# A fifth buffer for the high parts of the expert weights, and splits four tiles ahead of TensorE instead of three

## The reference

```python
logits = (h @ router).astype(jnp.float32)
top_v, top_i = lax.top_k(logits, TOP_K)          # 2 of 8 experts
gates = jax.nn.softmax(top_v, axis=-1)
...
for e in range(N_EXPERTS):
    y = y + gate_full[..., e:e + 1] * _swiglu(h, w_gate_up[e], w_down[e])
```

## Time and profile before

| what | value |
|---|---|
| median of 3 runs | 1521.85 us (1520.17 to 1522.1) |
| the profiled execution | 1522.17 us |
| its span, first to last instruction | 1520.2 us |
| busy share of the span: PE, PEld, DVE, ACT, POOL | 97%, 80%, 76%, 65%, 9% |
| granted clock of TensorE, mean | 0.998 |
| moved by DMA | 468.26 MB, mean 308 GB/s |
| item 0 begins on TensorE, item 7 ends | 617.2 us, 1508.6 us |

### The profile page before, as it was taken

The page is one execution under the profiler, slowest core; times in us unless marked ns, Lnnn a source line. Parts: engine busy times, 40 slices in busy tenths (PEclk is TensorE's granted clock), DMA queues, the critical chain, the costliest instruction groups (busy, mean ns, idle before and its releaser), DMA issues.

```text
span 1520.2 us, 19543 instructions
## 1 busy us (share of the span) xinstructions
PE 1481.3 (97%) x7678; PEld 1208.7 (80%) x7678; DVE 1158.3 (76%) x1021; ACT 991.1 (65%) x869; POOL 132.2 (9%) x137
## 2 busy tenths in 40 slices
PE   8999999999989999999999999999999999999996
PEld 6888888899969987888777788777888777888774
DVE  5555445454565456899899988899898999898997
ACT  5544434343453337777798777888776888776986
POOL 0000000006034314000000200000100000000000
PEclk9999999999999999999999999999999999999999
DMA  9655555567516653899999999999999999999996
GB/s 333 214 170 190 168 192 171 189 192 224 194 57 213 206 185 126 329 356 355 366 405 417 398 407 405 395 408 415 399 408 403 395 408 415 399 404 408 393 391 220
DMA packets 151056, 468.26 MB, mean 308 GB/s; under 512 B 9856, under 2 KB 15872, under 8 KB 138416
## 3 DMA queue, kind: packets, MB, share of 16 engines
q1 hardware_dynamic: 144784, 453.93, 79.8%
q0 software_dynamic: 2816, 9.96, 2.3%
q10 hardware_dynamic: 3360, 3.06, 0.7%
HBM read 459.55 MB, written 7.37 MB: 307 GB/s over the span
## 4 chain that ended last, share of the span: by engine, by line
PE 79%; DVE 13%; ACT 3%; DMA 1%; SPq 1%; issue 1%; DVEq 0%; ACTq 0%
DVE wlo L418 9%; PE bS L437 6%; PE bS L438 6%; PE bS L436 6%; PE bY L436 6%; PE bY L438 6%; PE bY L437 6%; PE bG L436 4%; PE bG L438 4%; PE bU L436 4%; PE bG L437 4%; PE bU L438 4%; PE bU L437 4%; DVE wlo_more L418 2%; ACT whi L412 2%
## 5 line engine op out<-in xcount | busy, mean ns | idle before, releaser
L418 DVE TENSOR_TENSOR wlo<-raw,whi 128x2048 fp32r<-128x2048 f32 x364 | 827.2, 2296 | 179.6 <-ACT whi L412 178.4
L412 ACT ACTIVATE whi<-raw 128x2048 fp32r<-128x2048 f32 x364 | 692.3, 1915 | 262.1 <-PE bS L438 118.2
L418 DVE TENSOR_TENSOR wlo_more<-raw_more,whi 128x2048 fp32r<-128x2048 f32 x60 | 136.4, 2288 | 10.7 <-ACT whi L412 10.6
L412 ACT ACTIVATE whi<-raw_more 128x2048 fp32r<-128x2048 f32 x60 | 114.5, 1914 | 28.0 <-DMA raw_more<-in_m_w_gate_up_dram 8.4
L1086 PE MATMUL bY<-whi,hTh 128*128 128x512 f32 x224 | 91.5, 408 | 6.9 <-DVE wlo L418 4.9
L436 PE MATMUL bY<-whi,hTh 128*128 128x512 f32 x224 | 89.8, 401 | 0.0
L437 PE MATMUL bY<-whi,hTl 128*128 128x512 f32 x224 | 89.1, 398 | 0.0
L437 PE MATMUL bS<-whi,eTl 128*128 128x512 f32 x192 | 76.4, 398 | 0.0
L436 PE MATMUL bS<-whi,eTh 128*128 128x512 f32 x192 | 76.4, 398 | 0.0
L1086 PE MATMUL bS<-whi,eTh 128*128 128x512 f32 x192 | 76.3, 398 | 0.0
L1087 PE MATMUL bY<-wlo,hTh 128*128 128x512 f32 x184 | 73.2, 398 | 0.0
(11 more groups left out here) (536 smaller groups left out, 3336.4 us busy)
## 6 DMA issues: line engine op xcount, KB each, us to landing
raw<-in_m_w_gate_up_dram SPq DMA_DIRECT2D x184, 1024.0 KB, 14.5
raw<-in_m_w_down_dram SPq DMA_DIRECT2D x90, 1024.0 KB, 14.4
raw_more<-in_m_w_gate_up_dram SPq DMA_DIRECT2D x40, 1024.0 KB, 14.6
raw<-in_b_w_in_dram SPq DMA_DIRECT2D x36, 1024.0 KB, 5.1
raw<-in_f_w_gate_up_dram SPq DMA_DIRECT2D x28, 1024.0 KB, 5.2
raw_more<-in_m_w_down_dram SPq DMA_DIRECT2D x20, 1024.0 KB, 14.2
raw<-in_f_w_down_dram SPq DMA_DIRECT2D x14, 1024.0 KB, 5.0
raw<-in_a_w_out_dram SPq DMA_DIRECT2D x4, 1024.0 KB, 16.8
```

Source lines behind the costliest of these rows:

```text
L412: nc.scalar.activation(whi[:, h], raw_of(r), ACT.Copy).then_inc(hi_done, 1)
L418: nc.vector.tensor_tensor(wlo_of(r), raw_of(r), whi[:, h].bitcast(F32), ALU.subtract).then_inc(lo_done, 1)
```

## The change

`whi` gets a fifth place, `whi_late`, in the memory of `hn`. The fifth place comes into use with tile `T_LATE + 1` = 97, that is tile 6 of item 0: until `T_LATE` = 96 the places go round by four, from there by five (`hi_slot`), and the wait for a free place looks back five tiles instead of four (`hi_free`). Tile 97's split also waits until `hn` has been stored and gathered from. In the experts ACT and DVE split tile t + 4 (`LEAD`) where they split tile t + 3, between the same small operations; one split of each (tile `T_MOE + 3`) is put ahead of item 0. SP's loops read the number of the next expert one tile later; the loads and their order are the same. Items beyond the eighth keep four places.

```diff
+LEAD = 4
@@ memory
+        top[0] = at_hn
+        whi_late = place("whi_late", [2048], F32R)
+        assert top[0] == phase
@@ places
+        T_LATE = -(-(T_MOE + HI + 1) // HI) * HI
+
+        def hi_slot(t):
+
+            return t % HI if t < T_LATE else (0, HI, 1, 2, 3)[(t - T_LATE) % (HI + 1)]
+
+        def hi_free(t, item):
+
+            if isinstance(item, int) and in_order(t, item) > T_LATE:
+                return used_count(t, item, HI + 1)
+            return used_count(t, item, HI)
+
+        whi_of = lambda h: whi[:, h] if h < HI else whi_late[:]
@@ slots
-                return ring(t), t % HI
+                return ring(t), hi_slot(t)
@@ make_hi
-                act.wait_ge(tile_used, used_count(t, item, HI))
-            nc.scalar.activation(whi[:, h], raw_of(r), ACT.Copy).then_inc(hi_done, 1)
+                act.wait_ge(tile_used, hi_free(t, item))
+            if isinstance(item, int) and in_order(t, item) == T_LATE + 1:
+                act.wait_ge(hn_out, 32)
+                act.wait_ge(gd_psum, 4)
+            nc.scalar.activation(whi_of(h), raw_of(r), ACT.Copy).then_inc(hi_done, 1)
@@ wblk_backward (what TensorE reads)
-            return backward(whi, h * 2048 + b * 512, HI * 2048), low
+            high = backward(whi, h * 2048 + b * 512, HI * 2048) if h < HI else backward(whi_late, b * 512, 2048)
+            return high, low
@@ SP
-            for t in range(FFN_TILES, FFN_TILES + CUT):
+            for t in range(FFN_TILES, FFN_TILES + LEAD):
...
-                for t in range(CUT, FFN_TILES):
+                for t in range(LEAD, FFN_TILES):
@@ ACT and DVE, ahead of item 0
             cut_tokens(0)
+            make_hi(act, T_MOE + LEAD - 1)
...
             ahead(T_MOE - 1)
+            make_lo(dve, T_MOE + LEAD - 1)
@@ full_item, and likewise half_item, of ACT and of DVE
-                        if not alone or t + CUT < FFN_TILES:
-                            make_hi(act, T_MOE + t + CUT, n)
+                        if not alone or t + LEAD < FFN_TILES:
+                            make_hi(act, T_MOE + t + LEAD, n)
```

More of the change, by code:

```diff
@@ L417, in make_lo @@
             dve.wait_ge(hi_done, count(item, FFN_TILES, t + 1))
-            nc.vector.tensor_tensor(wlo_of(r), raw_of(r), whi[:, h].bitcast(F32), ALU.subtract).then_inc(lo_done, 1)
+            nc.vector.tensor_tensor(wlo_of(r), raw_of(r), whi_of(h).bitcast(F32), ALU.subtract).then_inc(lo_done, 1)
         def wblk(t, b):
@@ L1420, in pre_tile_hi @@
                 r, h = slots(t, n)
-                act.wait_ge(tile_used, used_count(t, n, HI))
+                act.wait_ge(tile_used, hi_free(t, n))
                 act.wait_ge(pre_full, 16)
-                nc.scalar.activation(whi[:, h, 0:1024], raw_of(r)[:, 0:1024], ACT.Copy).then_inc(pre_hi, 1)
+                nc.scalar.activation(whi_of(h)[:, 0:1024], raw_of(r)[:, 0:1024], ACT.Copy).then_inc(pre_hi, 1)
                 act.wait_ge(*full_count(t, n))
-                nc.scalar.activation(whi[:, h, 1024:2048], raw_of(r)[:, 1024:2048], ACT.Copy).then_inc(hi_done, 1)
+                nc.scalar.activation(whi_of(h)[:, 1024:2048], raw_of(r)[:, 1024:2048], ACT.Copy).then_inc(hi_done, 1)
             def last_tile_hi(t, n):
                 r, h = slots(t, n)
-                act.wait_ge(tile_used, used_count(t, n, HI))
+                act.wait_ge(tile_used, hi_free(t, n))
                 for b in range(4):
@@ L1433, in last_tile_hi @@
                     sl = slice(b * 512, b * 512 + 512)
-                    nc.scalar.activation(whi[:, h, sl], raw_of(r)[:, sl], ACT.Copy).then_inc(last_hi if b < 3 else hi_done, 1)
+                    nc.scalar.activation(whi_of(h)[:, sl], raw_of(r)[:, sl], ACT.Copy).then_inc(last_hi if b < 3 else hi_done, 1)
             def turned_sel(n):
@@ L1485, in ahead @@
                     for t in tiles:
[L1486 to L1491, removed]
+                        if by_half and t + LEAD == FFN_TILES - 1:
+                            last_tile_hi(T_MOE + t + LEAD, n)
+                        elif by_half and t + LEAD == FFN_TILES - 2:
+                            pre_tile_hi(T_MOE + t + LEAD, n)
+                        elif not by_half or t + LEAD < FFN_TILES:
+                            make_hi(act, T_MOE + t + LEAD, n)
                 def copy_gate(j):
@@ L1588, in _ @@
                     y_right((m, 1, E - 1))
-                    for t in range(CUT):
+                    for t in range(LEAD):
                         make_hi(act, T_MOE + t, (m, 1, E))
@@ L2015, in pre_tile_lo @@
                 dve.wait_ge(pre_hi, 1)
-                nc.vector.tensor_tensor(wlo_of(r)[:, 0:1024], raw_of(r)[:, 0:1024], whi[:, h, 0:1024].bitcast(F32),
+                nc.vector.tensor_tensor(wlo_of(r)[:, 0:1024], raw_of(r)[:, 0:1024], whi_of(h)[:, 0:1024].bitcast(F32),
                                         ALU.subtract).then_inc(pre_lo, 1)
                 dve.wait_ge(hi_done, t + FFN_TILES * n + 1)
-                nc.vector.tensor_tensor(wlo_of(r)[:, 1024:2048], raw_of(r)[:, 1024:2048], whi[:, h, 1024:2048].bitcast(F32),
+                nc.vector.tensor_tensor(wlo_of(r)[:, 1024:2048], raw_of(r)[:, 1024:2048], whi_of(h)[:, 1024:2048].bitcast(F32),
                                         ALU.subtract).then_inc(lo_done, 1)
@@ L2027, in last_tile_lo @@
                     sl = slice(b * 512, b * 512 + 512)
-                    nc.vector.tensor_tensor(wlo_of(r)[:, sl], raw_of(r)[:, sl], whi[:, h, sl].bitcast(F32),
+                    nc.vector.tensor_tensor(wlo_of(r)[:, sl], raw_of(r)[:, sl], whi_of(h)[:, sl].bitcast(F32),
                                             ALU.subtract).then_inc(last_lo if b < 3 else lo_done, 1)
@@ L2063, in ahead @@
                     for t in tiles:
-                        if not alone or t + CUT < FFN_TILES:
-                            make_lo(dve, T_MOE + t + CUT, n)
+                        if not alone or t + LEAD < FFN_TILES:
+                            make_lo(dve, T_MOE + t + LEAD, n)
                         amid(t)
@@ L2106, in ahead @@
                     for t in tiles:
[L2107 to L2112, removed]
+                        if by_half and t + LEAD == FFN_TILES - 1:
+                            last_tile_lo(T_MOE + t + LEAD, n)
+                        elif by_half and t + LEAD == FFN_TILES - 2:
+                            pre_tile_lo(T_MOE + t + LEAD, n)
+                        elif not by_half or t + LEAD < FFN_TILES:
+                            make_lo(dve, T_MOE + t + LEAD, n)
                         amid(t)
```

## The result

The changed kernel took 1524.84 us in the median of 10 runs (1522.71 to 1528.2), the kernel before beside it 1521.95 us in 10 (1519.8 to 1522.63). The ratio is 1.0021, with a 95% interval of 1.0012 to 1.003, so in this set of runs the change costs some 2 to 4.5 us. The forecast was 1521.9, no change. What happened is the second rival in its place, at a price that the rival left half of out.

What follows compares the result with a forecast made beforehand. The load stream (404 to 405 GB/s) and the pace of TensorE and VectorE were taken to bind equally. All terms summed to 0 on the 1520.2 us span, so the median stayed 1521.9 us; range 1518.0 to 1524.6.

Steps and rivals of the forecast that it cites:

- the second rival: Item 7, last turn: ACT's up-half copy behind one more landing makes it slower, 1524.8 to 1526; over 3 us: chance 0.10.
- Two limits on each other: Experts, one full plus one half item: DMAs need all 222.3 us, and TensorE and VectorE need the same by their pace.
- So of the 8.8 us I count 0: Four half items: 2.2 us less VectorE work each, but the load stream takes it back; 0 counted, 8.8 the far end.
- The rule weighed: Half items: recurring 0.33 us waits a tile as a sign of too few buffers; by that alone, the full saving.
- The end, "the landing does not move": Item 7: tile 37 lands at 1493.0 and TensorE then runs through to the last tile; neither moves, 0 us.
- Extra wait of tile 97: Tile 6 of item 0: the store lands by 617.7, the split stands at 625.97; cover 8 us, cost 0.
- first split: The split put ahead of item 0 was ACT's and DVE's first in item 0 before, following the same operations: 0.
- SP's register: SP's register read one tile later: SP stands in its own full queue, each issue taking 2.4 us, so 0.
- Hidden, with 0.3 us to spare: 0, at worst 2.9: Item 7: last turn starts 2.9 us later, tile 29 at 1481.3; TensorE catches up by tile 37 at 1497.32.
- the term for a slower clock: Item 7 after the last turn: no clock term is written out; TensorE is taken to go at 1.87 us a tile.
- No more split ahead than before: Third rival: waits for `tile_used` or landings hold the fourth tile back, the lead stays at three; 1521.9, inside the forecast.

Runs made afterwards that it cites:

- Light loads alone: Kernel before with the experts' loads cut to 3/4 of their bytes (all but item 7's last two tiles): 1520.04 us, 0.9982 of before.
- both together: Changed kernel with the experts' loads cut to 3/4 of their bytes in the same way: 1504.34 us, 0.9885 of before.
- the lead given back: Changed kernel, but item 7 skips one turn of the lookahead on ACT and VectorE at tile 24: 1521.21 us, 0.9995 of before.
- the busy kernel: Kernel before with item 7's last up-half copy one split later, plus 12 spare matmuls on TensorE before the last turn: 1522.49 us, 0.9998 of before.

## Why the prediction was wrong, point by point

- **Two limits on each other: right.** Light loads alone leave items 1 to 6 as they are, the lead alone leaves items 3 to 6 as they are, both together take 15.7 us off. Equal rates in unequal items, and the time from issue to landing, showed it in the profile of before.
- **"So of the 8.8 us I count 0": right in its result, mis-sized in its far end.** 2.3 us came in item 1, and 1.5 of them were spent again in items 2 to 6; the likely reason, not tested, is that item 1 could live on loads that had landed early. The 2.2 us a half item are really 4.0 where landings are out of the way: beside one low part less, waits between the engines seem to go. In item 5 with light loads ACT waits 1.6 us instead of 5.1 for TensorE at its copies of `bS`, and VectorE 2.1 instead of 3.2 for the high parts.
- **The rule weighed.** With full loads the rows decide against it: the gaps of VectorE's pace go, and waits for landings take their place. With light loads it holds, at 4.0 us a half item, 3.3 in the last. The Trainium skill, Perfetto Trace Analysis, section Optimization Strategy, names too few buffers as a possible cause of recurring gaps; that was one cause here, with a second one as long behind it.
- **The end, "the landing does not move": right about the landing.** TensorE no longer hung on it.
- **Extra wait of tile 97, first split, SP's register, all 0: nothing in the runs speaks against them.** Item 0 takes 122.4 us as before, and 891.2 us with the lead given back leaves them no room; each was not tried alone.
- **The failed step: "Hidden, with 0.3 us to spare: 0, at worst 2.9".** Its times are right to 0.1 us: with the clock held, tile 29 starts at 864.0 us of the stretch, where the forecast's 1481.3 is 864.1 (1481.3 - 617.2), and the lateness is hidden. But I let TensorE go on at full clock after a stop of 3 us, and the term for a slower clock was put at nothing without a reason. What the half clock adds in after's profile: 3.65 - 1.97 = 1.7 us in the turn, and tile 29 takes 3.26 (1484.44 - 1481.18) instead of 1.96 (1480.32 - 1478.36, and 1481.05 - 1479.09 in the busy kernel), 1.3 more. 3.0 less the 0.3 to spare is 2.7; the profiles show 2.5 (893.66 - 891.15). The trace of before could have warned me: far ahead of the experts it has such a fall itself, shown in the last section.
- **The rival** had the place and, by luck, the size (1524.8 to 1526). Its condition was another: a second landing or a wait in item 6. Neither came.
- **No more split ahead than before: wrong.** The half items start with one more tile ready, and their VectorE time falls.

## What to carry to other kernels

A wait of 3 us on TensorE is not priced by whether the end catches up with it. In a stretch where it has run at full clock, a stop of that length can bring several microseconds at half the clock behind it, and that must fit into the slack too. When a lookahead is deepened, every small operation written between the splits goes later by one split, on every engine; walk the whole chain through them (here silu, product, copy, turn), not its last link, and give the lead back where slack is short. And when two limits lie on each other, neither change alone shows what it is worth: make the other limit light in an experiment first.

## What the runs showed of the hardware

My forecast had no price for a fall of the granted clock after a single stop. At item 7's last turn it went from 1.00 to 0.50 in every profile in which TensorE stood still for 2.55 to 3.4 us (four profiles), and in none in which it stood at most 0.6 us there (the seven others of the table). In after's profile it stayed down for some 6.8 us, through which TensorE was busy 6.22 of 6.70 us. Twelve matmuls whose results nobody uses, 2.9 us long, kept it up. The Trainium skill, TensorE: Matmul & The Clock Gate, section Why this matters for your kernels, warns of pauses of TensorE between bursts of matmuls, since they bring the slow clock back; the runs agree, and the price of one pause here was 1.6 to 2.9 us on the experts.

What shorter stops do is in the same traces, in other places. The kernel before, 19 us into its span: a stop of 1.76 us, then matmuls at the wide spacing, and the window behind it (PEclk after the five engines):

```profile
20.76 0.50 PE L436 MATMUL bG<-whi,xTh 128*128 128x512 f32 x1 [1.76 <-DVE xTl L1649]
...
21.76 0.63 PE L436 MATMUL bG<-whi,xTh 128*128 128x512 f32 x1
22.19 0.63 PE L437 MATMUL bG<-whi,xTl 128*128 128x512 f32 x1
```

```profile
21.40:24.40 3.00, 3.00 (x9) 2.33 (x8) 2.82 (x4) 1.33 (x4) 0.00 (x0) 0.50 1.06 394
```

All stops of TensorE longer than 1.2 us, from its first matmul to the experts' end, in the thirteen profiles (before, after and the eleven experiments), by what the granted clock did within 4 us behind them:

| stop of TensorE | stops | the clock fell to 0.50 |
|---|---|---|
| 1.27 to 1.29 us | 39 | 0 |
| 1.39 to 1.70 us | 36 | 1 |
| 1.76 to 2.15 us | 9 | 4 |
| 2.55 to 3.42 us | 7 | 7 |

So three microseconds are not needed: of the stops of some 2 us about half were enough, while one of 2.15 us was not, and one of 1.70 us was enough in one profile and not in the twelve others at the same place. What decides between them was not tested.
